# State weights, conv projection, layer norm and weight scaling placed differently in a hybrid conv and S5 encoder block on Trainium2

## The reference

```python
z = _rms_norm(h, norm_mix_g)                 # h: 16 meta tokens + x, 1024 channels
p = z @ w_in                                 # columns: conv value 512 | conv gate 512 | S5 input 512
u = p_value * sigmoid(p_gate)
y = depthwise_conv(u, conv_w, width=31) + conv_b
conv_out = silu(_layer_norm(y, ln_g, ln_b))  # over 512 channels
# S5: 32 groups x 16 channels, 64 complex states, forward and backward scan
# states_t = lam_bar * states_(t-1) + b_bar @ u_t ; y = Re(c @ states), directions summed
y = gelu(y + d_skip * u_ssm)
ssm_out = y * sigmoid(y @ glu_w + glu_b)
h = h + concat(conv_out, ssm_out) @ w_out
h = h + square(relu(_rms_norm(h, norm_ffn_g) @ w_ff1)) @ w_ff2
return _rms_norm(h, norm_final_g)[:, 16:, :]
```

## Time and profile before

| | before |
|---|---|
| median of 3 runs | 968.26 us (965.91 to 969.02) |
| profiled execution | 966.53 us |
| its span on the slowest core | 965.5 us (cores 955.3 to 965.5) |
| PE busy | 791.9 us, 82% |
| DVE busy | 517.2 us, 54% |
| ACT busy | 366.7 us, 38% |
| POOL busy | 379.8 us, 39% |

### The profile page before, as it was taken

How to read it: one execution, slowest core, us unless ns; L and a number is a source line. 1 busy time by engine, 2 the same in 40 slices (tenths; PEclk the granted TensorE clock), 3 DMA queues, 4 the chain that set the end, 5 groups by cost and what they waited for, 6 DMA issues and landing times.

```text
span 965.5 us, 15712 instructions; the slowest of 8 cores (955.3 to 965.5 us)
## 1 busy us (share of the span) xinstructions
PE 791.9 (82%) x4584; PEld 392.2 (41%) x4584; DVE 517.2 (54%) x975; ACT 366.7 (38%) x597; POOL 379.8 (39%) x419
## 2 busy tenths in 40 slices
PE   0466566879771788759999999999999999999992
PEld 0233333335420456514554444444444444444440
DVE  5968754652888960636663433443344334433577
ACT  5767665432210443586663111111111111111343
POOL 4868750881678640200004243323323342333130
PEclk9979787899985799969999999999999999999997
DMA  8588652546119917469905050410405050220034
GB/s 239 142 212 219 121 121 83 120 77 90 21 37 108 114 17 131 120 169 240 256 3 88 1 88 1 66 23 6 83 1 88 1 87 2 39 50 1 36 121 194
DMA packets 71955, 87.27 MB, mean 90 GB/s; under 512 B 7584, under 2 KB 55840, under 8 KB 71872
## 3 DMA queue, kind: packets, MB, share of 16 engines
q1 hardware_dynamic: 56752, 66.18, 29.8%
q0 software_dynamic: 14400, 19.76, 12.6%
q10 hardware_dynamic: 720, 0.33, 0.1%
HBM read 86.56 MB, written 19.45 MB: 110 GB/s over the span
## 4 chain that ended last, share of the span: by engine, by line
PE 65%; DVE 14%; issue 9%; DMA 3%; ACT 3%; SPq 3%; POOL 2%; DVEq 1%; ACTq 0%; POOLq 0%
PE p_pb L1135 23%; PE p_pb L1155 22%; PE p_pb L1081 6%; PE p_pb L833 4%; PE p_pb L442 3%; SPq L162 3%; DVE p_pb L470 3%; PE p_pb L1004 2%; DMA s_xt<-xl 2%; DVE s_vo L470 2%; PE p_pb L683 1%; DVE s_cd L470 1%; PE p_pb L922 1%; PE p_pb L933 1%; PE p_pb L935 1%
## 5 line engine op out<-in xcount | busy, mean ns | idle before, releaser
L470 DVE TENSOR_TENSOR s_h<-s_h,p_pb 128x512 f32<-128x512 f32 x288 | 197.7, 687 | 251.5 <-PE p_pb L1155 246.2
L470 POOL TENSOR_TENSOR s_hid<-s_rl 128x512 bf16<-128x512 f32 x128 | 133.6, 1047 | 320.6 <-ACT s_rl L1143 316.2
L1155 PE MATMUL p_pb<-s_w2c,s_hid 128*128 128x512 bf16 x1024 | 226.9, 379 | 4.4 <-DVE s_h L470 4.4
L1135 PE MATMUL p_pb<-s_zf,s_w1c 128*128 128x512 bf16 x1024 | 226.4, 379 | 0.0
L1143 ACT ACTIVATE s_rl<-p_pb 128x512 f32<-128x512 f32 x128 | 76.1, 597 | 328.0 <-PE p_pb L1135 320.1
L1155 PEld LDWEIGHTS p_pb<-s_w2c,s_hid 128*128 128x128 bf16 x1024 | 99.5, 98 | 126.7 <-issue 8.2
L1135 PEld LDWEIGHTS p_pb<-s_zf,s_w1c 128*128 128x128 bf16 x1024 | 100.1, 98 | 120.1
L833 PE MATMUL p_pb<-s_zsl,s_winv 128*128 128x512 bf16 x256 | 64.0, 410 | 17.6 <-ACT s_ust L455 9.8
L442 PE MATMUL p_pb<-s_zsl,s_winu 128*128 128x512 bf16 x256 | 72.2, 435 | 0.1
L372 PE MATMUL p_pb<-s_ident,s_zt 128*128 128x128 bf16 (+1 forms) x264 | 23.6, 242 | 29.8 <-ACT s_zt L358 29.8
L833 PEld LDWEIGHTS p_pb<-s_zsl,s_winv 128*128 128x128 bf16 x256 | 25.7, 104 | 55.0 <-issue 31.4
(11 more groups left out here) (169 smaller groups left out, 979.4 us busy)
## 6 DMA issues: line engine op xcount, KB each, us to landing
s_xt<-xl SPq DMA_DIRECT2D x32, 512.0 KB, 6.0
s_h<-xl SPq DMA_DIRECT2D x16, 512.0 KB, 18.2
s_w1c<-w_ff POOLq DMA_DIRECT2D x8, 1024.0 KB, 8.9
s_w2c<-w_ff POOLq DMA_DIRECT2D x8, 1024.0 KB, 10.5
out<-s_h SPq DMA_DIRECT2D x15, 512.0 KB, 2.7
s_wstv<-w_in SPq DMA_DIRECT2D x4, 1024.0 KB, 10.3
s_kf<-scr_rs SPq DMA_DIRECT2D x8, 384.0 KB, 16.4
s_wstu<-w_in SPq DMA_DIRECT2D x4, 512.0 KB, 11.3
```

Of the source, the lines that this page charges most:

```text
L470: op(eng, lambda e: e.tensor_tensor(o, a, b_, op=o_), r=r, w=w)
L1135: op("pe", lambda e, k=k, f=f: e.matmul(pb[pi_][:, :], w1c[fc % 2][:, k, f * 128:(f + 1) * 128], zf[:, k, b * 512:(b + 1) * 512], start=(k ...
L1155: op("pe", lambda e, f=f, half=half: e.matmul(pb[pi_][:, :], hid[hb][:, f, ti * 128:(ti + 1) * 128], w2c[fc % 2][:, f, half * 512:(half + ...
```

## The change

The edits, all in one version:

- `xt3` gets a place of its own (the later `sgt`/`usc` space), so that all 33 tiles go round four buffers and `load(n + 4)` is issued in each iteration.
- The scaling of `winu` and `winv` moves from DVE to ACT: `winu` in iterations 2 and 3, `winv` one row block in each of iterations 8, 9, 11, 12, 14, 15, 16, 17, and its four 1 MB loads at 4, 7, 10, 13.
- `px_setup` and `misc` are pushed at n = 12; in `px_setup` one factor and two temporaries are put in PSUM bank 2 (two more small copies for each of its five products), and the 8 small products of `misc` become one.
- State weights of direction 0 are made from n = 17 to 23, and what is left from n = 26 on (buffer set 1); `cw_pump` issues 3 operations per two tiles up to n = 24, with a third temporary pair, and again from n = 26.
- No `vg_chunk` in the tile loop: four in the loop right behind it, twelve under the scan, with `uc_read` of each batch as soon as it is there.
- `ln_stats` before all `ys_out`; `ln_norm` becomes `ln_sub` (DVE, 16) and `ln_mul` (DVE, 16, each followed by two POOL instructions of 128x256 that apply gain and offset); SiLU runs without pointers, 16 instructions of 128x512. All `ys_out` alternate between banks 0/1 and 6/7.

```diff
-    XT = [sb("xt%d" % i, [128, D], F32, VV2 + 4096 * i if i < 3 else UO + 12288) for i in range(4)]
+    XT = [sb("xt%d" % i, [128, D], F32, VV2 + 4096 * i if i < 3 else SG) for i in range(4)]
-    xbuf = [n % 4 if n < 17 else (n - 16) % 3 for n in range(33)]
+    xbuf = [n % 4 for n in range(33)]
...
+            fv = pb[2][:, 256:320].rearrange("p (r u) -> p r u", r=2)
+            op(eng, lambda e: e.tensor_copy(fv[:, 0], pq_re[:, f, :]), r=["pq_re"], w=["pb2"])
+            op(eng, lambda e: e.tensor_copy(fv[:, 1], pq_im[:, f, :]), r=["pq_im"], w=["pb2"])
+            x1, yr = [pb[2][:, 128 * j:128 * j + 32 * n].rearrange("p (k u) -> p k u", u=NU) for j in range(2)]
+            x2, yi = ptx[0][:, 0:n, :], ptx[1][:, 0:n, :]
...
-    def ln_norm(i):
...
+    def ln_mul(i):
+        yk = "yv%d" % i
+        y2 = yv[:, 2 * i:2 * i + 2, :]
         r2 = pb[5][:, 0:256].unsqueeze(1).to_broadcast([128, 2, 256])
         tt("dve", y2, y2, r2, ALU.mult, [yk, "pb5"], [yk])
+        for g in (2 * i, 2 * i + 1):
+            op("pool", lambda e, g=g: e.tensor_scalar(yv[:, g, :], yv[:, g, :], lnv[:, 1, g:g + 1], lnv[:, 2, g:g + 1], op0=ALU.mult, op1=ALU.add),
+               r=[yk, "lnv"], w=[yk])
 
     def ln_silu(i):
-        yk = "yv%d" % i
-        for dg in range(2):
-            g = 2 * i + dg
-            op("act", lambda e, g=g: e.activation(sil[:, g, :], yv[:, g, :], AF.Silu, bias=lnv[:, 2, g:g + 1], scale=lnv[:, 1, g:g + 1]),
-               r=[yk, "lnv"], w=["sil%d" % (g // 8)])
+        op("act", lambda e: e.activation(sil[:, 2 * i:2 * i + 2, :], yv[:, 2 * i:2 * i + 2, :], AF.Silu), r=["yv%d" % i], w=["sil%d" % (i // 4)])
...
     def winv_scale(k):
-        op("dve", lambda e: e.tensor_scalar(winv[:, k, :], wstv[k // 2 % 2][:, k % 2, :], pv[:, k:k + 1], None, op0=ALU.mult),
+        op("act", lambda e: e.activation(winv[:, k, :], wstv[k // 2 % 2][:, k % 2, :], AF.Identity, scale=pv[:, k:k + 1]),
...
-        if n == 21:
-            push(px_setup, 180)
+        if n == 12:
+            push(px_setup, 350)
             push(misc, 100)
+        if n in WVS:
+            winv_scale(WVS.index(n))
...
-            if n >= 5 and wb_list and len(bg) < 4 and (len(wb_list) > 8 or n > 13):
+            if n >= 5 and wb_list and len(bg) < 4 and len(wb_list) > 8:
                 do_wb(0)
-            pump(3600 if n in (7, 8, 12, 13) else 4200)
+            pump(3600 if n % 2 == 0 else 4300)
...
-            if 0 < n < 22:
-                cw_pump(2 if n < 21 else len(cq), 0)
-            if n < 25 and len(bg) < 4 and wb_list:
+            if n < 25:
+                if n in (20, 24):
+                    while cq:
+                        P.op(*cq.pop(0))
+                else:
+                    cw_pump(2 if n % 2 else 1, 0 if n < 20 else 2)
+            if n < 24 and len(bg) < 4 and wb_list:
                 do_wb(0)
...
-                cw_pump(2, 1)
-            if vq and n >= 22 and n % 2 == 0:
-                vg_chunk(*vq.pop(0), (1, 5))
+                cw_pump(2 if n % 2 else 1, 1)
...
-        if vq and nv < 3:
-            vg_chunk(*vq.pop(0), (1, 5))
+        if vq and nv < 4:
+            vg_chunk(*vq.pop(0), (1, 5), lambda: pump(3500))
...
     while vq:
+        if nb == 0:
+            uc_read(0)
+        kb = vq[0]
         vg_chunk(*vq.pop(0), ((0, 1), (2, 3))[nb % 2], lambda: vpump(10))
         nb += 1
+        if kb[2] == 3:
+            after(2, lambda b=kb[1]: uc_read(b))
         tick()
     tick()
-    for b in range(4):
-        uc_read(b)
+    tick()
...
-    for i in range(4):
-        ys_out(i, (0, 1))
-    ln_stats(2, 3)
+    ln_stats(2, 3)
+    for i in range(4):
+        ln_sub(i)
     for i in range(16):
-        ln_norm(i)
+        ln_mul(i)
+        if i + 4 < 16:
+            ln_sub(i + 4)
...
+    for i in range(8):
+        ys_out(i, (0, 1) if i % 2 == 0 else (6, 7))
     back_read("ys", 3, mixs, "mixs3")
+    for c in range(4):
+        yc_out(c)
```

More of the change, by code:

```diff
@@ L637, in _build @@
         P.place("cw%d" % i, "cw", CWO + 8704 * (i % 4), 8704)
-    ct = [(sb("cta%d" % k, [128, 4, 17, 16], F32, (VV1, UF)[k]), sb("ctb%d" % k, [128, 4, 17, 16], F32, (VV1, UF)[k] + 4352))
-          for k in range(2)]
+    ct = [(sb("cta%d" % k, [128, 4, 17, 16], F32, (VV1, UF, ZS + 7680)[k]), sb("ctb%d" % k, [128, 4, 17, 16], F32, (VV1, UF, ZS + 7680)[k] + 4352))
+          for k in range(3)]
     def cw_quad(i, ri, eng, st_):
@@ L1219, in misc @@
         op("dve", lambda e: e.tensor_copy(maskb[:], maskf[:]), r=["maskf"], w=["maskb"])
[L1220 to L1221 removed]
+        tt("dve", dmsk[:], maskf[:].unsqueeze(1).to_broadcast([128, 8, 16]), dcol[:].unsqueeze(2).to_broadcast([128, 8, 16]),
+           ALU.mult, ["maskf", "dcol"], ["dmsk"])
     bg = []
@@ L1234, in pump @@
             budget -= c
+            while late and any(k == late[0][1] for k in g[3]):
+                late.pop(0)[0]()
             P.op(*g)
@@ L1240, in winu_scale @@
         for k in range(8):
-            op("dve", lambda e, k=k: e.tensor_scalar(winu[:, k, :], wstu[:, k, :], pv[:, k:k + 1], None, op0=ALU.mult),
+            op("act", lambda e, k=k: e.activation(winu[:, k, :], wstu[:, k, :], AF.Identity, scale=pv[:, k:k + 1]),
                r=["wstu%d" % (k // 2), "pv"], w=["winu%d" % k])
@@ L1262, in _build @@
     nv = 0
-    wb_list = [(1, m, q) for q in range(4) for m in range(2)] + [(0, m, q) for q in range(4) for m in range(2)]
+    wb_list = [(1, m, q) for m in range(2) for q in range(4)] + [(0, m, q) for m in (1, 0) for q in range(4)]
     cw_list = [(i, ri) for i in (4, 5, 6, 7, 0, 1, 2, 3) for ri in range(2)]
@@ L1281, in _build @@
         kind, b, q = tiles[n]
-        ahead = [m for m in (n + 3, n + 4) if 4 <= m < NT and m not in loaded and (m < 17 or m <= n + 3)]
-        for m in ahead:
-            if m < 17 or m - 3 <= n:
-                loaded.add(m)
-                load(m)
+        if n + 4 < NT:
+            load(n + 4)
         trans(n, "act" if n % 2 or n < 7 else "dve")
@@ L1293, in _build @@
         while late:
-            late.pop(0)()
+            late.pop(0)[0]()
         if uq:
@@ L1297, in _build @@
             u_chunk(kd, ub, c, "act")
+        if n in (2, 3):
+            for g in wuq[4 * (n - 2):4 * (n - 2) + 4]:
+                P.op(*g)
         if n == 4:
@@ L1330, in _build @@
                 if nv == 8:
-                    assert not wb_list
                     push(far_tab, 100)
```

102 lines of the change are left out of this document (45 added, 57 removed).

## The result

The change makes the kernel faster by about half of what was forecast. The changed kernel takes 954.8 and 952.3 us, the kernel before 965.9 to 969.0 (968.3 in the middle); the ratio is 0.9853, with a 95% interval of 0.9804 to 0.9903, so about 14.2 us less than 968.3. The forecast was 938.7 us, 29.6 less, with a range of 922 to 955: the result lies at its upper edge, the direction is right and the size is not. (Executions in which the cores of one die ran at a lower clock and took longer are left out of every time in this document.)

A forecast was written before the change was run, and what follows sets the result against it. The prediction took the landing of the last mixc piece as the bound, with engines ahead of it waiting for each other. Its sum was 966.5 - 29 (loop) + 3.5 (scan) - 4 (norm) = 937, or 938.7 us on the median's scale, range 922 to 955.

The forecast's parts named there:

- What bounds the kernel: Whole kernel: only the last mixc landing at 442.1 us counts, since PE is busy without a gap from there.
- tiles 9 to 16: Tile loop: winv scales move to ACT, which becomes densest; hardly below 38 us; gain 2 us (loss 3 to gain 5).
- tiles 17 to 22: Tile loop: four xt buffers, px_setup gone; 5.0 us per tile, 30 instead of 36.0; gain 6 us (0 to 9).
- 22 to 25: Tile loop: two chunks go, state-weight batches come; 24 instead of 36.5 us; gain 12.5 us (8 to 17).
- The rival of the half clock (951): Tile loop: PE at half clock sets the pace, 0.75 us more in each of 16 tiles; 951 us, chance 0.15.
- The rival of the whole excess (921): Tiles 22 to 32: the chunks' whole excess comes back, 40.9 us instead of 23.5; 921 us, chance 0.17.
- Tiles 27 to the end of the loop: Loop's end: gain 11 us for tiles 26 to 32, less 3.6 for four chunks behind the loop instead of three.
- tiles 0 to 8: Tile loop's start: winu scales leave DVE but delay ACT; gain 1 us (0 to 5).
- Scales and `px_setup`: Tile loop: scale moves gain 1 and 2 us; px_setup counted at nothing, between 2 us lost and 2 gained on DVE.
- Under the scan: Scan to convolution: chunk products and late uc reads delay the convolution; 3.5 us later (0 to 12).
- Norm and SiLU: S5 output: last GELU 6.1 us earlier, 2 back at half clock; gain 4 (2 to 6); POOL norm 0.6 us each, hidden.
- the rule as the forecast has it: px_setup: a VectorE instruction with two SBUF inputs contends with GpSimd reading SBUF; one with at most one does not.

The follow-up runs named there:

- late_one: Changed kernel with at most one batch of state-weight rows transposed per iteration, where up to two were; 938.4 us, ratio 0.9694.
- experiment 6: Changed kernel, still up to two batches per iteration, their transposes going to banks 6 and 5 in turn; 939.8 us, ratio 0.9709.
- experiment 3: Kernel before with only the value and gate chunks taken out of the tile loop; 960.95 us, ratio 0.9925.
- scales_back: Changed kernel, two batches per iteration still allowed, with only the scaling of both input weights back on VectorE; 952.5 us, ratio 0.9833.
- experiments 10 and 13: Changed kernel with scaling of both input weights back on VectorE: with one batch per iteration 938.5 us, with two still allowed 952.5 us.
- experiment 9: Changed kernel with the four batches of uc read back together behind the last value and gate chunk, as before; 965.6 us, ratio 0.9966.
- tail_only: Kernel before with only the norm, S5 output and SiLU part of the change; 962.1 us, ratio 0.9941.
- late1_act: Changed kernel with one batch per iteration, and from tile 26 on even tiles' transposes evicted by ScalarE too; 934.75 us, ratio 0.9648.

## Why the prediction was half right

**What bounds the kernel.** That the chain ends with the last `mixc` piece held. It lands at 427.7 us instead of 442.1. The link back from it, and the start of PE behind it:

```profile
424.28 3.40 DMA s_mixc<-scr_yc
...
427.82 9.96 PE p_pb L1080 x33
```
```profile
428.19 1.91 PE L1080 MATMUL p_pb<-s_wout,s_mixs 128*128 128x512 bf16 x4
429.90 1.91 PE L1080 MATMUL p_pb<-s_wout,s_mixc 128*128 128x512 bf16 x4
...
433.29 1.03 PE L1080 MATMUL p_pb<-s_wout,s_mixc 128*128 128x512 bf16 x4
434.16 1.03 PE L1080 MATMUL p_pb<-s_wout,s_mixs 128*128 128x512 bf16 x4
```

Of the 14.4 us by which it lands earlier, 2.6 are lost again: PE had paused 3.9 us, three groups of four matmuls take 1.9 us and not 1.03, and 11.8 remain in the span. The forecast had 2 us for this.

**Tiles 9 to 25: the step that failed.** It was the time per tile taken from engines' sums: "can hardly fall below 38 us" and "Gain 2 us" for tiles 9 to 16, "I take 5.0, near the 5.1 and 4.5 of iterations without a chunk" for tiles 17 to 22, and "6.0 us per tile" for 22 to 25. The forecast divided ScalarE's busy time by the tiles and counted the state-weight batches as work of VectorE with one eviction each. It did not ask how many batches end in one iteration. Two of them share bank 6, and its eviction stands behind two 1.1 us instructions of ScalarE, the first of which may itself wait. The trace of before had this pattern in sight, in its steps of 9.8, 9.0 and 8.0 us, but only the steps of the earlier trace rows were looked at, which have chunks in them. The first of the three, at tile 8 to 9:

```profile
52.13 1.01 PE L628 MATMUL p_pb<-s_ident,s_wsr 128*128 128x128 bf16 x8 [6.21 <-ACT s_wb L632]
```

Tiles 9 to 22 were to gain 8 and lost 5.3, and 22 to 25 gained 3.8 instead of 12.5. With one batch per iteration and nothing else different the three terms are 3.5, 4.2 and 9.4, and the loop gains 30.0 where the forecast had 29: the sum over the engines' work came out in total, and what it left out was worth 15 us. The agreement of 938.4 with 938.7 us is luck in part: the terms miss by up to 3 us each with both signs, and about 3 us of that trace's loop are the short wait for the x tile.

**The rival of the half clock (951)** has the right symptom. Chunks of `u` take 3.0 to 3.6 us in the double iterations and the clock is 0.71 in tiles 17 to 22. But it named the wrong cause: not PE's work per tile but the wait ahead of it. In `late_one` the clock is 0.94, 0.89 and 0.87 in the same three stretches, with the same work. The Trainium skill (TensorE: Matmul & The Clock Gate, section "HAM oscillation — how this bites in real kernels") describes gaps between matmuls that bring the clock down; this trace agrees, with 3.4 to 5.0 us of wait ahead of the slow chunk in each of the four double iterations. Chunks of 3.6 us also stand behind shorter waits (at 104.4 us, behind 2.5 and 1.8), and in tiles 9 to 16 most of the doubles' cost goes with the wait while the granted clock stays at 0.80 (experiment 6).

**The rival of the whole excess (921)** had the chunks' iterations fall to the length of their neighbours, which makes 37.3 us (40.9 less 3.6) from `norm_z` 23 on. With the chunks alone moved (experiment 3) this part is 20.9 us shorter, and the steps there that had a chunk take 5.7 to 8.4 us.

**Tiles 27 to the end of the loop** gained 9.6 (forecast 7.4), and tiles 0 to 8 4.1 (forecast 1, between 0 and 5). The reason given for the latter, the `winu` scales, is not it: with the scales back on VectorE (`scales_back`) `norm_z` 9 still starts at 53.7. What went is the double step at tile 8, and it came back one tile later.

**Scales and `px_setup`.** The 3 us for tiles 0 to 16 rested on the scales, and their move is worth nothing (experiments 10 and 13). `px_setup` was counted at nothing, and no run contradicts it, but the trace has two waits less and two others in their place: see the last section.

**Under the scan** the first convolution pair comes 66.2 us behind the scan's start instead of 62.5, 3.7 us later (forecast 3.5). But the convolution itself then takes 62.6 instead of 59.9 us to the statistics, since DVE, not PE, sets its pace and came later with its weights: the third `cd_gen` starts 8.3 us behind the first pair instead of 5.7, and PE waits 9.2 us in all for `s_cd` instead of 6.1. That makes 6.3 us in all, where the forecast had 3.5 and no term for the second half. Its bound of 12, for all reads together, was not reached: that is the price when they stand at the end, which experiment 9 puts at 11 us.

**Norm and SiLU.** The two rows of the changed kernel by form, with mean ns of one and idle time before:

```profile
L971 POOL TENSOR_SCALAR s_yv<-s_yv,s_lnv 128x256 f32<-128x256 f32 x32 | 17.5, 557 | 20.5 <-DVE s_yv L470 18.3 <-POOL s_yv L971 2.2
...
L975 ACT ACTIVATE s_sil<-s_yv 128x512 bf16<-128x512 f32 x16 | 9.7, 626 | 1.1
```

The norm on POOL takes 0.56 us an instruction (forecast 0.6) and is hidden. The eight groups of S5 output follow at 3.3 us, 26.1 in all, and SPq issues for 31 us behind the last GELU. From the statistics to the first matmul behind `mixc` 8.8 us are gained (71.1 to 62.3), less 2.6 of half clock: 6.2, where the forecast had 6.1 - 2 = 4 and `tail_only` shows 5.7. The steps were right; 5.7 lies within the range of 2 to 6 and 6.2 just above it.

**What stays open.** By how much `late1_act` is faster than `late_one`, since its gain of 4.1 us in the loop is not in the span of its profiled execution; whether the four remaining loop edits have the last 1.5 us, which is within the intervals; and why one batch per iteration gives 4 us in one kernel and 15 in the other. That VectorE's work hid the rest in the kernel before is argued from its waits there. No run spread the state weights in the kernel before and nothing else, or put the eviction of bank 6 ahead of `norm_z`.

## What to carry to other kernels

A stage in which no engine is dense is bound by order and by shared buffers. So list, for each step, which of its instructions use the same PSUM bank and what the engine that empties the bank does first. An average over the step hides it, and one step that takes twice as long as its neighbours shows it. When work is taken out of a loop, ask what reads its result and when: moving the chunks gained 21.6 us in the loop and kept 2.7 of them at the next stage until the reads moved too. Of edits made together, some may lose what others win: here the chunks alone ended the loop 9.5 us earlier than the whole change did. The same defect cost 4 us in the kernel before, where another engine was dense, and 15 us in the changed one, so look for it after each gain, not only before.

## What the runs showed of the hardware

Two copies of `px_setup` in the timeline of DVE after, with the neighbour between them, all of 128x288 and from SBUF to SBUF:

```profile
94.30 2.11 DVE L579 COPY s_pxre<-s_pq_re 128x288 f32<-128x288 f32 x1
...
96.33 0.30 DVE L580 TENSOR_SCALAR s_pximx<-s_pq_im 128x288 f32<-128x288 f32 x1
96.39 2.24 POOL L470 TENSOR_TENSOR s_cta<-s_pwre,s_cmat 128x1088 f32<-128x1088 f32 x1
...
96.73 2.07 DVE L581 COPY s_pximx<-s_pq_im 128x288 f32<-128x288 f32 x1
```

The copies take 2.1 us and the scale of the same shape 0.30. Each copy ends within 0.2 us of the end of the POOL instruction beside it (96.2 and 98.6 us). In the kernel before, the same two copies took 0.31 us each. The forecast spoke only of products with two SBUF inputs: two of these took 2.10 and 2.45 us there, and with one input in PSUM all take 0.18 to 0.30. So what `px_setup` gained at its products it lost again at its copies. The Trainium skill (SBUF — State Buffer, section "Who interferes with whom") says that a copy in a two-port mode and a GpSimd instruction exclude each other for a whole instruction, which is what these two rows look like; the rule as the forecast has it leaves this case out, in which one SBUF input is enough.

Loads of an x tile (512 KB) land 5.9 us after their issue in the median; one took 15.8 us, when 1 MB of weights, the read of `uf` and other x tiles were under way together.
